# Exponentials as a step of their own on ScalarE, a transposition one unit forward, and another order of units in the output projection

## The reference, cut to what matters

```python
for layer in range(DEPTH):                      # DEPTH = 2
    h = rms_norm(x, norm_g[layer])
    proj = h @ w_in[layer]                      # 1024 -> 3584
    o_sb  = stick_breaking(sb_q, sb_k, sb_v) * silu(sb_g)      # 6 heads of 64
    o_mb  = moba(rope(mb_q), rope(mb_k), mb_v) * silu(mb_g)    # 6 heads, causal softmax
    mkv   = rms_norm(mem, mem_norm_g[layer]) @ w_mem_kv[layer] # 256 memory rows
    o_mem = softmax(mem_q @ mk.T / 8) @ mv * silu(mem_g)       # 4 heads
    x = x + concat(o_sb, o_mb, o_mem) @ w_out[layer]
x = rms_norm(x, final_norm_g)
# second block, one layer; 16 meta tokens stand ahead of the rows
swa:  16 heads, softmax over a window, the meta keys and a sink value
diff: 8 heads, (softmax(q1 k1) - lam softmax(q2 k2)) v, then an RMS norm per head
h = h + rms_norm((g_swa * (o_swa @ w_branch_swa) + g_diff * (o_diff @ w_branch_diff)) @ w_out_2)
h = h + rms_norm((silu(u @ w_gate) * (u @ w_up)) @ w_ffn_out)
```

## Time and profile before

| | |
|---|---|
| median of 3 runs | 849.33 us (846.13 to 850.15) |
| the profiled execution's own time | 849.11 us |
| its span in the profile | 847.3 us |
| mean granted TensorE clock | 0.989 of full |
| TensorE (PE) busy | 807.4 us, 95% |
| VectorE (DVE) busy | 495.3 us, 58% |
| ScalarE (ACT) busy | 469.5 us, 55% |

### The profile page before, as it was taken

The page is one execution under the profiler, slowest core; times in us unless marked ns, Lnnn a source line. Parts: engine busy times, 40 slices in busy tenths (PEclk is TensorE's granted clock), DMA queues, the critical chain, the costliest instruction groups (busy, mean ns, idle before and its releaser), DMA issues.

```text
span 847.3 us, 12690 instructions
## 1 busy us (share of the span) xinstructions
PE 807.4 (95%) x4238; PEld 653.9 (77%) x4238; DVE 495.3 (58%) x731; ACT 469.5 (55%) x1004; POOL 130.0 (15%) x204
## 2 busy tenths in 40 slices
PE   7998999899999999889998999999999999999996
PEld 4777777677777786767777888788887888888884
DVE  5355556566465555856665657666686644455454
ACT  5676476455666654636664666564555533444352
POOL 2011021000234110343334252200000000000000
PEclk9999999999999999989999999999999999999999
DMA  8873543358864365552233344456675736566641
GB/s 256 258 184 110 164 151 105 132 162 262 259 202 125 117 226 170 147 137 84 63 91 96 104 122 143 150 152 224 222 243 176 225 121 191 161 192 186 207 137 50
DMA packets 147295, 137.78 MB, mean 163 GB/s; under 512 B 15025, under 2 KB 115649, under 8 KB 147233
## 3 DMA queue, kind: packets, MB, share of 16 engines
q1 hardware_dynamic: 145136, 129.89, 49.8%
q0 software_dynamic: 2096, 7.09, 2.9%
HBM read 135.90 MB, written 1.05 MB: 162 GB/s over the span
## 4 chain that ended last, share of the span: by engine, by line
PE 71%; ACT 7%; DVE 4%; issue 2%; POOL 1%; ACTq 0%; DVEq 0%; POOLq 0%
PE psum L1163 57%; PE psum L1141 6%; PE psum L1262 3%; ACT w_hi L1444 2%; PE psum L1397 2%; ACT probs L1571 2%; PE psum L1365 1%; PE psum L1183 1%; DVE w_lo L1640 1%; ACT p_t L1589 1%; POOL rtmp L1109 1%; DVE stats L1773 1%; PE psum L1323 0%; ACT xn L1477 0%; ACT gtmp L1614 0%
## 5 line engine op out<-in xcount | busy, mean ns | idle before, releaser
L1640 DVE TENSOR_TENSOR w_lo<-raw,w_hi 128x1024 fp32r<-128x1024 f32 (+1 forms) x234 | 270.1, 1174 | 127.9 <-ACT w_hi L1444 76.2
L1163 PE MATMUL psum<-w_hi,h_hi 128*128 128x512 f32 (+1 forms) x656 | 259.7, 396 | 3.5 <-DVE h_lo L1698 3.3
L1444 ACT ACTIVATE w_hi<-raw 128x1024 fp32r<-128x1024 f32 (+1 forms) x234 | 230.8, 1010 | 48.8 <-PE psum L1163 20.5
L1163 PE MATMUL psum<-w_lo,h_hi 128*128 128x512 f32 (+1 forms) x656 | 247.0, 377 | 0.0
L1163 PE MATMUL psum<-w_hi,h_lo 128*128 128x512 f32 (+1 forms) x656 | 246.4, 376 | 0.0
L1163 PEld LDWEIGHTS psum<-w_hi,h_hi 128*128 128x128 f32 x656 | 124.2, 189 | 30.1 <-issue 13.9
L1163 PEld LDWEIGHTS psum<-w_lo,h_hi 128*128 128x128 f32 x656 | 123.8, 189 | 19.2
L1163 PEld LDWEIGHTS psum<-w_hi,h_lo 128*128 128x128 f32 x656 | 124.5, 190 | 15.5
L1571 ACT ACTIVATE probs<-psum,stats 128x272 f32<-128x272 f32 (+2 forms) x104 | 47.3, 464 | 57.6 <-DVE stats L1765 25.6
L1163 PE MATMUL psum<-w_hi,m_hi 128*128 128x512 f32 x152 | 60.2, 396 | 2.4 <-DVE m_lo L1698 1.5
L1163 PE MATMUL psum<-w_lo,m_hi 128*128 128x512 f32 x152 | 59.3, 390 | 0.0
(11 more groups left out here) (171 smaller groups left out, 999.0 us busy)
## 6 DMA issues: line engine op xcount, KB each, us to landing
raw<-in_w_in SPq DMA_DIRECT2D x112, 256.0 KB, 3.7
raw<-in_w_ffn_in SPq DMA_DIRECT2D x88, 256.0 KB, 4.2
raw<-in_w_in SPq DMA_DIRECT2D x24, 512.0 KB, 4.4
raw<-in_w_out SPq DMA_DIRECT2D x24, 512.0 KB, 3.6
raw<-in_w_in SPq DMA_DIRECT2D x64, 192.0 KB, 2.7
raw<-in_w_ffn_out SPq DMA_DIRECT2D x22, 512.0 KB, 4.6
meta_w<-in_w_in SPq DMA_DIRECT2D x10, 1024.0 KB, 7.7
raw<-in_w_mem_kv SPq DMA_DIRECT2D x8, 512.0 KB, 3.7
```

The source lines that it names most:

```text
L1163: last = nc.tensor.matmul(psum[:, bank, 0:n], sx[name][:, c, t * P:(t + 1) * P], wx[:, kk, 0:n], start=u["first"] and kk == 0 and z == 0, ...
L1444: nc.scalar.activation(weights(u)[0][:, :, 0:n], raw[:, u["raw"], :, 0:n], ACT.Copy)\
L1640: nc.vector.tensor_tensor(lo[:, :, 0:n], raw[:, u["raw"], :, 0:n], hi[:, :, 0:n].bitcast(F32), ALU.subtract)\
```

## The change

There are three edits. First, `mb`, `mem` and `diff` get `soft` places half a unit behind their `scores`, and the condition on ACT now leaves the exponentials to `soft` for every kind but sb. TensorE's and DVE's parts stay in `scores`. Second, in layer 0 `turns[1]` comes with `turns[0]` after unit 1 of the mb group, and `turns[2]` stays alone after unit 2. Third, the output projection's units go a0 a1 b0 b1 a2 b2 instead of a0 a1 a2 b0 b1 b2, in both layers.

```diff
@@ SLOTS
-    "mb": dict(turn_qk=(2.5,), gate=(2.25, 4.25), scores=(3, 3), turn_p=(4.5, 5), out=(5.5, 7),
+    "mb": dict(turn_qk=(2.5,), gate=(2.25, 4.25), scores=(3, 3), soft=(3.5, 3.5), turn_p=(4.5, 5), out=(5.5, 7),
                turn_mix=(7.5,)),
-    "mem": dict(turn_qk=(1,), gate=(0.25, 2.25), scores=(1.75, 1.75, 4.25, 4.25), turn_p=(4, 5.25, 6.5, 7.5),
+    "mem": dict(turn_qk=(1,), gate=(0.25, 2.25), scores=(1.75, 1.75, 4.25, 4.25), soft=(2.25, 2.25, 4.75, 4.75),
+                turn_p=(4, 5.25, 6.5, 7.5),
                 out=(5.75, 6.75, 7.75, 8.75), turn_mix=(9.75,)),
...
-    "diff": dict(turn_qk=(1.5, 2.5), scores=(4.25, 4.25), blend=(6.25,), turn_p=(7.75,), out=(8.75,),
+    "diff": dict(turn_qk=(1.5, 2.5), scores=(4.25, 4.25), soft=(4.75, 4.75), blend=(6.25,), turn_p=(7.75,), out=(8.75,),
                  turn_mix=(9.75,)),
@@ make_plan
-            side(head_group(layer, "mb", 0), {0: mem_norm, 1: turns[:1], 2: turns[1:3], 3: turns[3:]})
+            side(head_group(layer, "mb", 0), {0: mem_norm, 1: turns[:2], 2: turns[2:3], 3: turns[3:]})
...
-        line.extend(("unit", u) for u in a[:3] + b[:3])
+        line.extend(("unit", u) for u in a[:2] + b[:2] + a[2:3] + b[2:3])
@@ build, block.scalar
-                    if (kind == "swa") != (what == "soft"):
+                    if (kind != "sb") != (what == "soft"):
```

## The result

The changed kernel takes **837.46 us** (median of 4 runs, 836.53 to 838.52) against 848.52 us for the kernel before (4 runs, 846.13 to 850.15): a ratio of 0.987, 95% interval 0.984 to 0.990. The forecast was 838.0. In the three later sets of experiments the kernel before has medians of 847.27 to 848.28 (15 to 23 runs each), so the change is worth 10 to 11 us. The profiled execution took 838.35 us with a span of 836.5.

The account below looks back on a forecast made before the run. TensorE bounds the kernel, busy 807.4 of 847.3 us; gains lie in its idle time and clock. 3.3 + 1.1 + 1.8 - 0.6 - 0.1 + 1.5 + 2.1 + 2.1 = 11.2 off 849.1 gives 837.9, forecast 838.0, range 834.3 to 844.5.

Parts of the forecast that it names:

- Memory turns: Layer 0: first `out` stops waiting, second waits about 0.5; gain 3.3 us, bounds 1.6 and 3.9.
- The 1.7 for the clock: Layer 0 memory turns: 1.7 us of the 3.3 gained by avoiding 3.4 us at half clock.
- the clock falls otherwise: Whole kernel: clock drops move; one more gives 839.7, one fewer 836.3; chance 0.64 shared with the forecast.
- Memory heads: Earlier weight split ends TensorE's waits: gain 1.1 us in layer 0, 1.8 in layer 1.
- swa to diff: Last swa group's `turn_tm`: `p_t` goes before the first diff head's exponentials, wait 2.36 to 0.25; gain 2.1 us.
- output projection: Layer 0: a2's wait behind the memory heads' `turn_mix` goes, covered by four half units; gain 1.5 us.
- The mb groups: Behind the memory heads: later exponentials delay `o_st`; cost 0.6 us in layer 1, 0.1 in layer 0.
- in layer 0 the same place has about 0.4 more room: Mb group behind layer 0's memory heads: 0.4 us more room than layer 1, where a new 0.6 wait was predicted.
- The 0.1 that I gave to the first mb group's `p_t`: First mb group: `p_t` comes late by what a `mix_lo` wait hides; cost 0.1 us, bounds 0 and 0.5.
- Differential heads: Squares ahead of the next head's exponentials end five `o_st` waits, 3.3 us; new waits leave a gain of 2.1.
- The predicted give-back: Differential heads: `blend` ends later, so `turn_p` waits 0.25 us anew, counted five times.
- slower: Differential heads: exponentials end too late for `blend`; 851.2 us, or 854.6 with clock losses; chance 0.05.

Follow-up runs that it names:

- the one with the split alone: Kernel before, with only one weight split per differential head, from the second on, moved behind the previous head's squares: 844.47 us against 847.27.
- The kernel without the rotation: Changed kernel with the differential heads' q and k rotation on POOL left out, a tiny copy standing in: 837.51 us against 848.28 for the kernel before.

## Why the prediction was right

*Memory turns.* The working holds step by step: the first `out` without a wait, the second 0.55 late against "about 0.5", 3.31 against 3.3. Half of it hung on chance. The 1.7 for the clock rests on the lower level following this wait, as in the earlier trace rows. The same wait of 2.16 to 2.17 is in seven of the profiles (before and six experiments), and the lower level follows in four. Window of the kernel with the output projection alone, then of the one with the split alone (length, busy times, granted clock, DMA share, GB/s):

```profile
71.50:74.90 3.40, 3.37 (x20) 2.95 (x21) 2.33 (x4) 1.80 (x4) 1.30 (x5) 1.00 0.02 6
```

```profile
71.30:78.10 6.80, 6.49 (x20) 5.38 (x21) 2.47 (x5) 2.08 (x5) 2.12 (x8) 0.51 0.27 80
```

The first stays at 2.4 GHz behind the wait, the second is at 1.2 GHz for twice the 3.4 us. In the six profiles without the wait no loss is at this place. So the place is worth 1.6 to 3.3, or 5 where the loss is double, by how the execution goes. For the total, the rival "the clock falls otherwise" describes it better than the forecast does: alone, this edit gave 1.0 (0.1 to 2.2), and that the profile before had its loss at this place is luck in the forecast's favour.

*Memory heads* in both layers, *swa to diff* and the *output projection* came to within 0.3 us. These are the places where one named instruction stood ahead of a named copy, with a row for each.

*The mb groups.* The step that failed is "in layer 0 the same place has about 0.4 more room": it cost 0.96. I had counted room from where `out` came, as in layer 1, and not followed the `w_lo` that DVE could not write in between; the `o_st` behind it frees the bank of a `turn_p` that waited 0.16 already, so there was no room at all. Nor had I seen the 0.23 that the same entry gains at 140.22. The 0.1 that I gave to the first mb group's `p_t` did not show: the lead stays at -1.75 there.

*Differential heads.* 3.3 less 5 times 0.25 gave 2.1, and 2.36 came, of which the stretch behind the last head took 1.2 back: 1.1 in all. The five waits for `o_st`, 3.3 in the list, are worth 4.1 by the start times (0.77 for one listed with 0.61, 1.05 for the one of 0.89). The predicted give-back, waits for `blend`'s probs, came at two heads of five (0.5 in all); at the others a wait for POOL, 0.2 to 0.4 at four heads, came ahead of it and made TensorE late enough. The kernel without the rotation shows that the forecast of a short wait at every head was right for what it looked at, and that POOL was missing from it. Also missing was what comes after the last head, an `xn` evacuation behind the last `blend`:

```profile
544.89 0.42 DVE L1699 TENSOR_TENSOR m_lo<-psum,m_hi 128x256 fp32r<-128x256 f32 x1
...
546.41 0.92 DVE L1804 SCALAR_TENSOR_TENSOR probs<-probs,rec 128x272 f32<-128x272 f32 x2
547.24 1.22 DVE L1641 TENSOR_TENSOR w_lo<-raw,w_hi 128x1024 fp32r<-128x1024 f32 x1
548.38 0.69 DVE L1867 COPY xn<-psum 128x512 f32<-128x512 f32 x1
```

DVE does `m_lo`, `blend`, a `w_lo` and then `xn` without a pause, and the `m_lo` waits for the splits behind the late exponentials. With the exponentials back at their scores 0.15 is lost here instead of 1.2.

*The total.* The two terms that failed, the mb group of layer 0 (0.86 too good) and the differential heads with what is behind them (0.96 too good), err the same way. The other steps make up 0.8 of it, the start, the clock and the wait for `x` 0.5, and the median of the four runs is 0.9 below the profiled one. That 837.9 and 837.46 agree to 0.4 us is in part luck; the steps agree less well. The rival "slower", with `blend` behind TensorE, was right on the slack (1.6) and wrong on what holds `blend`: against TensorE's own progress the exponentials start 3.2 later (4.7 ahead of the `o_st` transposes before, 1.4 now) and `blend` ends 1.3 later.

## What to carry to other kernels

When a step on ACT or DVE stands ahead of something late, list all that stands between, and move the piece with the most slack: here a weight split whose use was two units away, not the exponentials that a `blend` waits for. An edit that is right for one kind of group (diff, mem) can cost more than it brings in another (mb), and only place-by-place leads show it where medians don't. A wait read in one profile is worth its idle time at its place, and the clock behind it only at times. A kernel with one suspect taken out shows what that suspect had hidden: without POOL's work TensorE waited for `blend` instead, and the time stayed.

## What the hardware showed

**The clock.** Two executions of one program differ in where the granted clock falls to half. The lower level (0.50 of full, 1.2 GHz) began between 8 and 14 us in seven of thirteen profiles, for no difference in the instructions there, behind the same wait of 2.16 us in four of seven, and behind the equally unchanged wait of 2.36 us at the last `turn_tm` in one of six. Each such stretch lasts 3.4 us or twice that. The Trainium skill ("TensorE: Matmul & The Clock Gate", section "What's actually happening") says of a program's first matmuls that the moment at which the clock changes varies, because it depends on where in a freely running window they land. These rows are of later places, of which it does not say this; a loss that comes and goes behind an unchanged wait fits. Such a loss is no ground for 1.7 us of a forecast.

**DVE and POOL.** A POOL product of 128x128 takes 0.46 us alone and 1.17 to 1.18 beside a `w_lo`, whose mean of 128x768 rises from 0.95 to 1.14 us over the heads and falls back when POOL's work is taken away. The Trainium skill ("SBUF — State Buffer", section "Who interferes with whom") says that a DVE instruction with two SBUF inputs contends with a GpSimd instruction that reads SBUF; `w_lo` reads `raw` and `w_hi`, both in SBUF, and the rows agree. In the kernel before one of a head's four POOL products of 128x128 is slowed in this way, with the changed order in most heads three (1.17 each), and the page's busy time of POOL grew by 5.5 us at the same 204 instructions.
